# Recurrent stage: five high halves on GpSimd, the exponentials ahead of the roots, one gate block ahead of a gate chunk

## The chip, the cores and the metric

The kernel runs on one core of a Trainium2 chip. The metric is the device time in microseconds, the median of three runs: 1562.83 (1562.11 to 1563.29).

## The reference, cut to what matters

Two transformer-like blocks of depth 2 run over 256 tokens of width 1024. The change touches one stage, the gated linear recurrence of the first block, and the projection behind it:

```python
gate_br, rec = jnp.split(h @ w_in, 2, axis=-1)
gate_br = gelu(gate_br);  xc = causal_depthwise_conv(rec, conv_w, conv_b)
r = sigmoid(block_diag_linear(xc, w_r, b_r));  i = sigmoid(block_diag_linear(xc, w_i, b_i))
log_a = -8.0 * r * softplus(-lam);  a = exp(log_a)
mult = sqrt(-expm1(2.0 * log_a));  u = mult * (i * xc)
hs = linear_recurrence(a, u)            # h = a_t * h + u_t
return (hs * gate_br) @ w_out
```

Everything is in fp32.

## The kernel before, in words

**Weights.** All weights pass through one stream of 576 units of 128x1024 fp32. A unit is loaded (in pairs, from SP's queue) into the ring `raw` of 8 slots. A high half `w_hi` of it is made by ScalarE (`split_hi`, L480 to L492, a Copy with output rounded to the matmul's format), and VectorE makes the low half `w_lo = raw - w_hi` (`split_lo`, L1018 to L1025). A product of a 128x128 block with 256 tokens is three matmuls: hi by hi (L1822), hi by lo of the operand (L1828), lo by hi (L1829). A load into a slot waits for the low halves of the slot's last pair; `split_hi` waits for the load and for TensorE to be done with the unit that held the slot 8 units earlier (the semaphore `unit_used`).

**Order.** Each engine has its own order, written out by hand. `pump_to(c)` on ScalarE and on VectorE makes the halves of all units up to c that aren't made yet; the calls stand between the stage's own steps.

**The stage.** Units `gates`+0 to +11 are: eight chunks of the gate projection (`gate_chunk`, 8 products each, units +0, 1, 2, 4, 8, 9, 10, 11), two units with the blocks of w_r (+3, +6) and two with those of w_i (+5, +7). `r_block(n)` and `i_block(n)`, n = 0 to 3, are 4 products each. Behind them come the `wout` units +0 to +7, 8 products each. TensorE's order is: chunks 0, 1, 2, r_block 0, chunk 3, r 1, i 0, r 2, i 1, r 3, i 2, chunk 4, i 3, chunk 5, chunks 6 and 7 interleaved by output bank, wout 0 to 7. `r_block(n)` needs `xc_lo(n)` of VectorE (L1336), wout k needs `y_lo(k // 2)` (L1389).

**ScalarE** does for each quarter n of the features: the high half of the convolved input (`xc_hi`, L651), the tanh of the r gate and of the i gate (L659, L664), tanh and exp for the decay (`r_tanh`, `decay`, L671, L676), the root (`mult_root`, L680), the gelu (L684) and the high half of the result (`y_hi`, L688). Tanh and exp share a function table; the root and the gelu each load one of their own.

**VectorE** does the convolution (L1349, 6 instructions a quarter), `xc_lo`, the scaled gate input (`mixed_in`, L1357), `mult_square` (L1364, L1365), `read_gate` (L1370, which reads a bank of the gate projection from PSUM), `recur` (L1377 and two scans, L1379), `y_full` (L1384) and `y_lo` (L1389). `y_full(b)` needs `gelu(b)`; `gelu(b)` needs `read_gate(b)`; `recur(b)` needs `mult_root(b)`.

**GpSimd** only issues a few DMAs and makes one sum of squares, later on (L446, L448).

Of the kernel before, what the change touches and what calls it, by code (L numbers as in the profile page):

```python
# [38 lines left out]
UNIT = 1024  # L39
RING = 8  # L40
# [117 lines left out]
GATE_UNITS = [AT["gates"] + _n for _n in (0, 1, 2, 4, 8, 9, 10, 11)]  # L158
R_UNITS = [AT["gates"] + _n for _n in (3, 6)]
I_UNITS = [AT["gates"] + _n for _n in (5, 7)]  # L160
STEPS = {"ffn0": 0, "ffn1": FFS, "ffn2": 2 * FFS, "ffn3": 3 * FFS, "mlp0": 4 * FFS, "mlp1": 4 * FFS + MLS}


class Signals:


    def __init__(self, sem):
# [10 lines left out]
        self.out_done = sem("out_done")  # L178

        self.hi_ready = sem("hi_ready")  # L180
        self.lo_ready = sem("lo_ready")
        self.unit_used = sem("unit_used")

# [130 lines left out]
def build(nc, stream, x_in, ctx_in, small, consts, late, poolmat, tab, out):  # L314
    with ExitStack() as es:
# [118 lines left out]
        @block.gpsimd  # L434
        def _(pool):
            gp = nc.gpsimd

            def sum_squares(n):

                m = POOL_SUMS[NORMS[n]]  # L440
                for b in range(1, 4):
                    pool.wait_ge(S.sq_ready, 4 * n + b + 1)
                    if b > 1:
                        pool.wait_ge(S.pool_sum, 3 * m + b - 1)
                    a = buf[4][:, half(0)]
                    gp.tensor_tensor(a, a, buf[4][:, half(b)], ALU.add).then_inc(S.pool_sum, 1)  # L446
                pool.wait_ge(S.pool_sum, 3 * m + 3)
                gp.tensor_tensor(buf[4][:, 0:T], buf[4][:, 0:T], buf[4][:, T:2 * T], ALU.add).then_inc(S.ctx_ssq, 1)  # L448


            pool.wait_ge(S.hi_ready, 4)
            pool.dma_start(cst[:, CC["tri"]:], consts[:, CC["tri"]:]).then_inc(S.mixer_consts_in, 16)
            for n, name in enumerate(NORMS):
                if name == "ctx":

                    pool.wait_ge(S.acc_ready, 4 * ACC["wout"] + 4)
                    pool.dma_start(buf[3][:, :], ctx_in).then_inc(S.ctx_in, 16)
                if name == "woe":

                    pool.wait_ge(S.acc_ready, 4 * ACC["ffn3"] + 4)  # L460
                    pool.dma_start(buf5[:, 0:NLATE], late).then_inc(S.late_in, 16)

                    pool.dma_start(buf[2][:, 0:TABW], tab[0]).then_inc(tab_in[0], 16)
                    pool.wait_ge(S.mixed_lo, 4)
                    pool.dma_start(buf[4][:, 0:TABW], tab[1]).then_inc(tab_in[1], 16)
                if name == "pool":

                    pool.wait_ge(S.na_max, 16)
                    pool.dma_start(buf[2][:, :], poolmat[:, 0:8 * T]).then_inc(S.poolmat_in, 16)
                    pool.dma_start(buf[0][:, 1024:2048], poolmat[:, 8 * T:]).then_inc(S.poolsum_in, 16)  # L470
                if name in POOL_SUMS:
                    sum_squares(n)
# [3 lines left out]
        def _(act):  # L476
# [2 lines left out]

            def split_hi(c):  # L480

                if c in MOD_UNIT:
                    return
                slot = c % RING
                act.wait_ge(raw_landed[slot // 2], 16 * (c // RING + 1))
                before = [n for n in range(c - RING, -1, -RING) if n not in MOD_UNIT]
                if before:

                    act.wait_ge(S.unit_used, SPLIT[before[0]] + 1)
                u = slice(slot * UNIT, (slot + 1) * UNIT)  # L490
                sc.activation(w_hi[:, u], raw[:, u], ACT.Copy).then_inc(S.hi_ready, 1)  # L491

            def pump_to(last):
                while nxt[0] <= min(last, UNITS - 1):
                    split_hi(nxt[0])
                    nxt[0] += 1
# [164 lines left out]
            def i_gate(n):  # L661
                act.wait_ge(S.i_ready, n + 1)
                for k in (2 * n, 2 * n + 1):
                    sc.activation(ig[:, k, :], bank2(n)[:, k % 2, :], ACT.Tanh, bias=ty("bih", k), scale=0.5).then_inc(S.i_read, 1)  # L664

            def r_tanh(n):
                if n == 0:
                    act.wait_ge(S.ms_psum, NRM["ffn0"] + 1)
                act.wait_ge(S.r_read, 2 * n + 2)
                for k in (2 * n, 2 * n + 1):  # L670
                    sc.activation(tn[:, k, :], r[:, k, :], ACT.Tanh, bias=ty("sp4", k), scale=ty("sp4", k)).then_inc(S.lru_tanh, 1)  # L671

            def decay(n):
                act.wait_ge(S.lru_tanh, 2 * n + 2)
                for k in (2 * n, 2 * n + 1):
                    sc.activation(r[:, k, :], r[:, k, :], ACT.Exp, bias=ty("nsp4", k), scale=ty("nsp4", k)).then_inc(S.lru_decay, 1)  # L676
# [5 lines left out]
            def gelu(b):  # L682
                act.wait_ge(S.acc_read, 4 * RD["gate"] + b + 1)
                sc.activation(buf[1][:, half(b)], buf[1][:, half(b)], ACT.Gelu_apprx_tanh).then_inc(S.gelu_done, 1)  # L684

            def y_hi(b):
                act.wait_ge(S.lru_y, b + 1)
                sc.activation(u_hi[:, 2 * b:2 * b + 2, 0:T], ck(buf[1])[:, 2 * b:2 * b + 2, :], ACT.Copy)\  # L688
                  .then_inc(S.operand_hi, 2)
# [1 line left out]
            xc_hi(0)  # L691
            pump_to(AT["gates"] + 7)
            xc_hi(1)
            pump_to(AT["gates"] + 8)
            sc.preload_act_table_set("exp_and_others")
            r_gate(0)
            r_tanh(0)
            xc_hi(2)
            pump_to(AT["gates"] + 9)
            r_gate(1)  # L700
            decay(0)
            xc_hi(3)
            i_gate(0)
            r_gate(2)
            pump_to(AT["gates"] + 10)
            i_gate(1)
            r_gate(3)
            r_tanh(1)
            i_gate(2)
            decay(1)  # L710
            r_tanh(2)
            i_gate(3)
            pump_to(AT["gates"] + 11)
            decay(2)
            r_tanh(3)
            decay(3)
            sc.preload_act_table_set("sqrt_and_others")
            mult_root(0)
            mult_root(1)
            gelu(0)  # L720
            pump_to(AT["wout"])
            y_hi(0)
            gelu(1)
            pump_to(AT["wout"] + 1)
            mult_root(2)
            mult_root(3)
            pump_to(AT["wout"] + 2)
            y_hi(1)
            gelu(2)
            gelu(3)  # L730
            pump_to(AT["wout"] + 3)
            pump_to(AT["wout"] + 5)
            y_hi(2)
            pump_to(AT["wout"] + 6)
            y_hi(3)
            pump_to(AT["ffn1"] + AHEAD - 1)
            gain_operand("ffn2_0", "wout", early=AT["ffn1"] + 8)
# [269 lines left out]
        def _(dve):  # L1007
# [10 lines left out]
            def split_lo(c):  # L1018

                if c in MOD_UNIT:  # L1020
                    modulate(c, *MOD_UNIT[c])
                    return
                dve.wait_ge(S.hi_ready, SPLIT[c])
                u = slice((c % RING) * UNIT, (c % RING + 1) * UNIT)
                ve.tensor_tensor(w_lo[:, u], raw[:, u], w_hi[:, u].bitcast(F32), ALU.subtract).then_inc(S.lo_ready, 1)  # L1025

# [43 lines left out]
            def pump_to(last):  # L1070
                while nxt[0] <= min(last, UNITS - 1):
                    split_lo(nxt[0])
                    nxt[0] += 1
# [281 lines left out]
            def mixed_in(b):  # L1355
                dve.wait_ge(S.i_read, 2 * b + 2)
                ve.scalar_tensor_tensor(buf[3][:, half(b)], buf[3][:, half(b)], 1.0, buf[0][:, half(b)], ALU.add, ALU.mult)\  # L1357
                  .then_inc(S.mixed_in, 1)

            def mult_square(b):  # L1360

                dve.wait_ge(S.lru_decay, 2 * b + 2)
                dve.wait_ge(S.mixed_in, b + 1)
                link(ve.tensor_tensor(buf[0][:, half(b)], buf[2][:, half(b)], buf[2][:, half(b)], ALU.mult))  # L1364
                ve.scalar_tensor_tensor(buf[4][:, half(b)], buf[0][:, half(b)], 1.0, buf[4][:, half(b)],  # L1365
                                        ALU.add, ALU.mult).then_inc(S.lru_m2, 1)
# [29 lines left out]
            mult_square(1)  # L1396
            pump_to(AT["gates"] + 11)
            mixed_in(2)
            mixed_in(3)
            mult_square(2)  # L1400
            mult_square(3)
            read_gate(0)
            recur(0)
            read_gate(1)
            y_full(0)
            pump_to(AT["wout"])
            y_lo(0)
            pump_to(AT["wout"] + 1)
            recur(1)
            read_gate(2)  # L1410
            y_full(1)
            pump_to(AT["wout"] + 2)
            y_lo(1)
            read_gate(3)
            recur(2)
            pump_to(AT["wout"] + 3)
            y_full(2)
            recur(3)
            y_lo(2)
            pump_to(AT["wout"] + 5)  # L1420
            y_full(3)
            pump_to(AT["wout"] + 6)
            y_lo(3)
            pump_to(AT["ffn1"] + AHEAD - 1)
            update_and_operand("wout", "ffn1", "ffn2_0", 1.0)
# [357 lines left out]
        def _(pe):  # L1783
# [257 lines left out]
            i_block(1, 0)  # L2041
            r_block(3, 1)
            i_block(2, 1)
            gate_chunk(4, 0)
            i_block(3, 0)
            gate_chunk(5, 2)

            unit_ready(GATE_UNITS[7])
            for n in range(NC):
# [571 lines left out]
```

## Time and profile before

| | before |
|---|---|
| time, median of 3 runs | 1562.83 us |
| span of the profiled execution (first to last instruction) | 1560.5 us |
| TensorE busy | 1523.2 us (98%) |
| VectorE busy | 1164.3 us (75%) |
| ScalarE busy | 785.1 us (50%) |
| GpSimd busy | 9.6 us, 15 instructions |
| mean granted TensorE clock | 0.995 |

The profiled execution's own time isn't given apart from the runs; its span is 2.3 us below their median, which is the time around the first and the last instruction. Busy time of TensorE is modelled from pipelined matmuls, so what counts there is where it stood idle. The recurrent stage lies between about 232 and 299 us of the span.

### The profile page before, as it was taken

How to read it: one execution, taken by the hardware profiler on the slowest of the kernel's cores; microseconds unless marked ns; L12 is line 12 of the kernel's file. 1: busy time of each engine (PE TensorE's matmuls, PEld its weight loads, DVE VectorE, ACT ScalarE, POOL GpSimd, SP SyncE). 2: the span in 40 equal slices, each digit the busy share in tenths (PEclk: the TensorE clock that was granted, in tenths of full speed). 3: DMA queues.
4: the chain of work that ended last, by engine and by line, in shares of the span. 5: the costliest groups of instructions: out<-in, count | busy, mean ns of one | idle time of the engine just before them, and what ended most of it. 6: DMA issues, size and time to landing. Idle time of an engine off the chain costs nothing.

```text
span 1560.5 us, 28953 instructions
## 1 busy us (share of the span) xinstructions
PE 1523.2 (98%) x11842; PEld 1463.9 (94%) x11842; DVE 1164.3 (75%) x1675; ACT 785.1 (50%) x1127; POOL 9.6 (1%) x15
## 2 busy tenths in 40 slices
PE   7999999999999999999989999999999999899998
PEld 7999998999999899999769999987799999899998
DVE  7887788978877858787767877774768887686563
ACT  5444458643435633445765343454654544454542
POOL 0000000000000100000000000000000000000000
PEclk9999999999999999999999999999999999999999
DMA  7656652646664537666233666643345767336540
GB/s 286 230 225 261 228 221 91 243 154 249 226 253 187 226 114 284 250 236 249 81 135 109 263 250 248 247 161 135 102 149 219 268 265 274 136 126 226 189 163 28
DMA packets 43735, 311.57 MB, mean 200 GB/s; under 512 B 4848, under 2 KB 5104, under 8 KB 6512
## 3 DMA queue, kind: packets, MB, share of 16 engines
q1 hardware_dynamic: 42048, 303.33, 51.7%
q0 software_dynamic: 1008, 5.73, 1.0%
q8 instruction: 75, 1.23, 0.3%
q10 hardware_dynamic: 576, 1.05, 0.2%
q14 instruction: 28, 0.23, 0.0%
HBM read 309.05 MB, written 1.05 MB: 199 GB/s over the span
## 4 chain that ended last, share of the span: by engine, by line
PE 67%; DVE 10%; ACT 3%; issue 1%; DVEq 0%; ACTq 0%
PE psum L1822 18%; PE psum L1828 18%; PE psum L1829 18%; DVE w_lo L1025 5%; PE psum L2066 3%; PE psum L2072 3%; PE psum L2071 3%; DVE buf L1034 2%; ACT w_hi L491 2%; PE psum L1899 1%; DVE buf L1195 1%; PE psum L2385 1%; PE psum L2396 0%; PE psum L2315 0%; DVE buf L1198 0%
## 5 line engine op out<-in xcount | busy, mean ns | idle before, releaser
L1822 PE MATMUL psum<-u_hi,w_hi 128*128 128x256 f32 (+1 forms) x2288 | 658.1, 288 | 17.1 <-DVE u_lo L1117 9.6
L1025 DVE TENSOR_TENSOR w_lo<-raw,w_hi 128x1024 fp32r<-128x1024 f32 x480 | 564.5, 1223 | 115.6 <-ACT w_hi L491 115.4
L1828 PE MATMUL psum<-u_lo,w_hi 128*128 128x256 f32 (+1 forms) x2288 | 650.1, 284 | 0.0
L1829 PE MATMUL psum<-u_hi,w_lo 128*128 128x256 f32 (+1 forms) x2288 | 649.9, 284 | 0.0
L491 ACT ACTIVATE w_hi<-raw 128x1024 fp32r<-128x1024 f32 x480 | 477.3, 1046 | 71.0 <-PE psum L1822 59.0
L1822 PEld LDWEIGHTS psum<-u_hi,w_hi 128*128 128x128 f32 x2288 | 440.9, 193 | 21.5 <-DVE w_lo L1025 9.7
L1828 PEld LDWEIGHTS psum<-u_lo,w_hi 128*128 128x128 f32 x2288 | 441.0, 193 | 0.4
L1829 PEld LDWEIGHTS psum<-u_hi,w_lo 128*128 128x128 f32 x2288 | 440.8, 193 | 0.0
L1822 PE MATMUL psum<-hid_hi,w_hi 128*128 128x256 f32 x1220 | 346.2, 284 | 1.8 <-issue 1.2
L1828 PE MATMUL psum<-hid_lo,w_hi 128*128 128x256 f32 x1220 | 345.2, 283 | 0.0
L1829 PE MATMUL psum<-hid_hi,w_lo 128*128 128x256 f32 x1220 | 345.1, 283 | 0.0
L1822 PEld LDWEIGHTS psum<-hid_hi,w_hi 128*128 128x128 f32 x1220 | 234.2, 192 | 2.4 <-issue 1.4
L1828 PEld LDWEIGHTS psum<-hid_lo,w_hi 128*128 128x128 f32 x1220 | 234.2, 192 | 0.1
L1829 PEld LDWEIGHTS psum<-hid_hi,w_lo 128*128 128x128 f32 x1220 | 234.2, 192 | 0.0
L549 ACT ACTIVATE buf<-buf 128x256 f32<-128x256 f32 x88 | 36.8, 418 | 313.3 <-DVE buf L1195 313.3
L1034 DVE SCALAR_TENSOR_TENSOR buf<-raw,tiny,buf 128x512 f32<-128x512 f32 x196 | 143.4, 748 | 4.9
L596 ACT ACTIVATE buf<-buf,tiny 128x256 f32<-128x256 f32 x64 | 29.1, 501 | 110.2 <-DVE buf L1260 110.2
L1195 DVE TENSOR_TENSOR buf<-psum,rstd 128x512 f32<-128x512 f32 x88 | 60.4, 686 | 22.1 <-PE psum L1829 21.6
L2066 PE MATMUL psum<-w_hi,u_hi 128*128 128x512 f32 x176 | 71.9, 408 | 0.9 <-DVE x L1135 0.9
L1198 DVE TENSOR_TENSOR buf<-buf 128x256 f32<-128x256 f32 x88 | 37.4, 425 | 42.6 <-ACT buf L549 42.6
L1200 DVE TENSOR_TENSOR hid_lo<-buf,hid_hi 128x256 fp32r<-128x256 f32 x88 | 37.4, 425 | 42.6 <-ACT hid_hi L551 42.6
L2072 PE MATMUL psum<-w_hi,u_lo 128*128 128x512 f32 x176 | 68.9, 391 | 0.0
(261 smaller groups left out, 1048.5 us busy)
## 6 DMA issues: line engine op xcount, KB each, us to landing
raw<-stream SPq DMA_DIRECT2D x288, 1024.0 KB, 5.0
buf<-tab POOLq DMA_DIRECT2D x2, 768.0 KB, 5.3
x<-x_in SPq DMA_DIRECT2D x2, 512.0 KB, 6.8
buf<-ctx_in POOLq DMA_DIRECT2D x1, 1024.0 KB, 9.4
buf<-poolmat POOLq DMA_DIRECT2D x1, 1024.0 KB, 5.3
out<-x ACTq DMA_DIRECT2D x4, 256.0 KB, 2.5
cst<-consts POOLq DMA_DIRECT2D x1, 864.0 KB, 9.0
buf<-late POOLq DMA_DIRECT2D x1, 640.0 KB, 4.2
```

The lines of the kernel that those rows point to most:

```text
L491: sc.activation(w_hi[:, u], raw[:, u], ACT.Copy).then_inc(S.hi_ready, 1)
L1025: ve.tensor_tensor(w_lo[:, u], raw[:, u], w_hi[:, u].bitcast(F32), ALU.subtract).then_inc(S.lo_ready, 1)
L1034: return ve.scalar_tensor_tensor(acc, w, c, acc, ALU.mult, ALU.add)
L1195: ve.tensor_tensor(t2.rearrange("p (k t) -> p k t", k=2), bank2(UP_BANK[j]), over2(rstd[:, :]), ALU.mult).then_inc(S.up_scaled, 1)
L1198: ve.tensor_tensor(h32[:, 0:T], sil, t2[:, T:2 * T], ALU.mult).then_inc(S.hid_f32, 1)
L1200: ve.tensor_tensor(ff_lo[:, j % 4, :], h32[:, 0:T], ff_hif[:, j % 4, :], ALU.subtract)\
L1822: ins = te.matmul(dst, w_hi[:, w], hi, start=first, stop=False, skip_group_check=True)
L1828: te.matmul(dst, w_hi[:, w], lo, start=False, stop=False, skip_group_check=True)
L1829: return te.matmul(dst, w_lo[:, w], hi, start=False, stop=last, skip_group_check=True)
L2066: ins = te.matmul(dst, u_hi[:, k, t], w_hi[:, w], start=first, stop=False)
L2071: te.matmul(dst, u_hi[:, k, t], w_lo[:, w], start=False, stop=False)
L2072: return te.matmul(dst, u_lo[:, k, t], w_hi[:, w], start=False, stop=last)
```

## The change

GpSimd makes the high halves of the units gates+8 to +11 and wout+0, as fp32 copies with the same waits; VectorE waits for GpSimd's semaphore for these. ScalarE no longer makes them. On ScalarE the order is now: all tanh and exp steps, then the four roots, then the gelus. On VectorE some steps trade places to go with that. On TensorE `i_block(3)` comes ahead of chunk 4.

```diff
+POOL_HI = [AT["gates"] + _n for _n in (8, 9, 10, 11)] + [AT["wout"]]
@@ gpsimd
+            def split_hi(c):
+                slot = c % RING
+                pool.wait_ge(raw_landed[slot // 2], 16 * (c // RING + 1))
+                before = [n for n in range(c - RING, -1, -RING) if n not in MOD_UNIT]
+                pool.wait_ge(S.unit_used, SPLIT[before[0]] + 1)
+                u = slice(slot * UNIT, (slot + 1) * UNIT)
+                gp.tensor_copy(w_hi[:, u], raw[:, u]).then_inc(S.pool_hi, 1)
+                if name == "ffn0":
+                    for c in POOL_HI:
+                        split_hi(c)
@@ scalar
-            pump_to(AT["gates"] + 8)        # likewise +9, +10, +11 further down
             ...
             i_gate(0)
             r_gate(2)
+            r_tanh(1)
             i_gate(1)
             r_gate(3)
+            decay(1)
             i_gate(2)
             r_tanh(2)
+            decay(2)
             i_gate(3)
             r_tanh(3)
             decay(3)
             sc.preload_act_table_set("sqrt_and_others")
             mult_root(0)
             mult_root(1)
+            mult_root(2)
+            mult_root(3)
             gelu(0)
-            pump_to(AT["wout"])
             y_hi(0)
+            pump_to(AT["wout"] + 1)
             gelu(1)
-            pump_to(AT["wout"] + 1)
-            mult_root(2)
-            mult_root(3)
-            pump_to(AT["wout"] + 2)
             y_hi(1)
+            pump_to(AT["wout"] + 3)
             gelu(2)
             gelu(3)
             ...
@@ vector
-                dve.wait_ge(S.hi_ready, SPLIT[c])
+                if c in POOL_HI:
+                    dve.wait_ge(S.pool_hi, POOL_HI.index(c) + 1)
+                else:
+                    dve.wait_ge(S.hi_ready, ACT_HI[c])
             ...
             mixed_in(2)
+            mult_square(2)
             mixed_in(3)
-            mult_square(2)
+            pump_to(AT["wout"])
+            read_gate(0)
             mult_square(3)
-            read_gate(0)
             recur(0)
+            y_full(0)
             read_gate(1)
-            y_full(0)
-            pump_to(AT["wout"])
             y_lo(0)
+            recur(1)
             pump_to(AT["wout"] + 1)
-            recur(1)
+            y_full(1)
             ...
@@ tensor
             i_block(2, 1)
-            gate_chunk(4, 0)
             i_block(3, 0)
-            gate_chunk(5, 2)
+            gate_chunk(4, 1)
+            gate_chunk(5, 1)
```

## Rows read from the trace of the kernel before

**Rows 1.** The page: TensorE's totals, and the chain that ended last.
```profile
PE 1523.2 (98%) x11842; PEld 1463.9 (94%) x11842; DVE 1164.3 (75%) x1675; ACT 785.1 (50%) x1127; POOL 9.6 (1%) x15
PE psum L1822 18%; PE psum L1828 18%; PE psum L1829 18%; DVE w_lo L1025 5%; PE psum L2066 3%; PE psum L2072 3%; PE psum L2071 3%; DVE buf L1034 2%; ACT w_hi L491 2%; PE psum L1899 1%; DVE buf L1195 1%; PE psum L2385 1%; PE psum L2396 0%; PE psum L2315 0%; DVE buf L1198 0%
```

**Rows 2.** Waits, 250 to 262 us, then 262 to 300 us: total, times, longest.
```profile
DVE w_lo L1025 <- ACT w_hi L491: 3.8, 2, 2.4
...
PE psum L1822 <- DVE u_lo L1389: 3.5, 1, 3.5
DVE w_lo L1025 <- ACT w_hi L491: 0.5, 1, 0.5
```

**Rows 3.** Windows: length, busy us (xcount) of each engine, PEclk, DMA share, GB/s.
```profile
267.40:270.80 3.40, 0.00 (x0) 0.00 (x0) 3.31 (x5) 2.80 (x5) 0.00 (x0) 0.87 0.00 0
270.80:276.70 5.90, 5.86 (x27) 5.89 (x28) 5.40 (x7) 4.68 (x7) 0.00 (x0) 0.50 0.50 174
276.70:297.10 20.40, 19.79 (x165) 19.61 (x164) 20.21 (x25) 13.86 (x16) 0.00 (x0) 1.00 0.57 208
```

**Rows 4.** Timeline of TensorE's matmuls: start, us, engine, line; idle before in brackets.
```profile
260.83 0.28 PE L1829 MATMUL psum<-u_hi,w_lo 128*128 128x256 f32 x1
261.37 0.39 PE L1822 MATMUL psum<-u_hi,w_hi 128*128 128x256 f32 x1 [0.26 <-DVE w_lo L1025]
```

**Rows 5.** Timeline of VectorE in the stage.
```profile
241.46 0.68 DVE L1336 TENSOR_TENSOR u_lo<-buf,u_hi 128x512 fp32r<-128x512 f32 x1
242.07 2.45 DVE L1349 SCALAR_TENSOR_TENSOR buf<-buf,prm 128x256 f32<-128x256 f32 x6
244.44 1.21 DVE L1025 TENSOR_TENSOR w_lo<-raw,w_hi 128x1024 fp32r<-128x1024 f32 x1
245.92 0.69 DVE L1336 TENSOR_TENSOR u_lo<-buf,u_hi 128x512 fp32r<-128x512 f32 x1 [0.27 <-ACT u_hi L651]
...
250.04 0.69 DVE L1336 TENSOR_TENSOR u_lo<-buf,u_hi 128x512 fp32r<-128x512 f32 x1
...
254.03 0.69 DVE L1364 TENSOR_TENSOR buf<-buf 128x512 f32<-128x512 f32 x1
254.75 0.69 DVE L1365 SCALAR_TENSOR_TENSOR buf<-buf 128x512 f32<-128x512 f32 x1
...
265.09 0.68 DVE L1370 TENSOR_TENSOR buf<-psum,rstd 128x512 f32<-128x512 f32 x1
...
297.02 1.28 DVE L1135 SCALAR_TENSOR_TENSOR x<-psum,x 128x512 f32<-128x512 f32 x2
```

**Rows 6.** Timeline of ScalarE in the stage.
```profile
258.27 0.84 ACT L664 ACTIVATE buf<-psum,tiny 128x256 f32<-128x256 f32 x2 [1.09 <-PE psum L1829]
259.00 1.06 ACT L491 ACTIVATE w_hi<-raw 128x1024 fp32r<-128x1024 f32 x1
...
265.63 1.28 ACT L684 ACT_TABLE_LOAD   x1
266.93 0.63 ACT L684 ACTIVATE buf<-buf 128x512 f32<-128x512 f32 x1
```

**Rows 7.** Timeline of GpSimd, then of VectorE, around 540 us.
```profile
539.95 4.17 POOL L446 TENSOR_TENSOR buf<-buf 128x512 f32<-128x512 f32 x3 [241.59 <-ACT buf L509]
544.20 1.60 POOL L448 TENSOR_TENSOR buf<-buf 128x256 f32<-128x256 f32 x1
...
538.86 1.23 DVE L1025 TENSOR_TENSOR w_lo<-raw,w_hi 128x1024 fp32r<-128x1024 f32 x1 [0.81 <-ACT w_hi L491]
540.88 2.79 DVE L1470 TENSOR_SCALAR buf<-psum,tiny 128x512 f32<-128x512 f32 x4 [0.80 <-PE psum L2072]
543.59 3.30 DVE L1025 TENSOR_TENSOR w_lo<-raw,w_hi 128x1024 fp32r<-128x1024 f32 x2
```

**Rows 8.** Windows of a later stage, columns as in rows 3.
```profile
1195.00:1196.80 1.80, 0.03 (x2) 0.03 (x1) 1.72 (x7) 0.05 (x1) 0.00 (x0) 1.00 0.94 314
...
1198.30:1201.70 3.40, 3.40 (x18) 3.40 (x18) 2.45 (x4) 3.28 (x4) 0.00 (x0) 0.50 0.02 5
```

More of the change, by code:

```diff
@@ L160 @@
 I_UNITS = [AT["gates"] + _n for _n in (5, 7)]
+POOL_HI = [AT["gates"] + _n for _n in (8, 9, 10, 11)] + [AT["wout"]]
+ACT_HI = []
+for _c in range(UNITS):
+    ACT_HI.append((ACT_HI[-1] if ACT_HI else 0) + (_c not in MOD_UNIT and _c not in POOL_HI))
 STEPS = {"ffn0": 0, "ffn1": FFS, "ffn2": 2 * FFS, "ffn3": 3 * FFS, "mlp0": 4 * FFS, "mlp1": 4 * FFS + MLS}
@@ L180, in __init__ @@
         self.hi_ready = sem("hi_ready")
+        self.pool_hi = sem("pool_hi")
         self.lo_ready = sem("lo_ready")
@@ L480, in split_hi @@
             def split_hi(c):
-                if c in MOD_UNIT:
+                if c in MOD_UNIT or c in POOL_HI:
                     return
@@ L698, in _ @@
             xc_hi(2)
-            pump_to(AT["gates"] + 9)
             r_gate(1)
@@ L704, in _ @@
             r_gate(2)
-            pump_to(AT["gates"] + 10)
+            r_tanh(1)
             i_gate(1)
             r_gate(3)
-            r_tanh(1)
+            decay(1)
             i_gate(2)
-            decay(1)
             r_tanh(2)
+            decay(2)
             i_gate(3)
-            pump_to(AT["gates"] + 11)
-            decay(2)
             r_tanh(3)
@@ L719, in _ @@
             mult_root(1)
-            gelu(0)
-            pump_to(AT["wout"])
-            y_hi(0)
-            gelu(1)
-            pump_to(AT["wout"] + 1)
             mult_root(2)
             mult_root(3)
-            pump_to(AT["wout"] + 2)
+            gelu(0)
+            y_hi(0)
+            pump_to(AT["wout"] + 1)
+            gelu(1)
             y_hi(1)
+            pump_to(AT["wout"] + 3)
             gelu(2)
             gelu(3)
-            pump_to(AT["wout"] + 3)
+            pump_to(AT["wout"] + 4)
+            y_hi(2)
             pump_to(AT["wout"] + 5)
-            y_hi(2)
-            pump_to(AT["wout"] + 6)
             y_hi(3)
@@ L1398, in _ @@
             mixed_in(2)
+            mult_square(2)
             mixed_in(3)
-            mult_square(2)
+            pump_to(AT["wout"])
+            read_gate(0)
             mult_square(3)
-            read_gate(0)
             recur(0)
+            y_full(0)
             read_gate(1)
-            y_full(0)
-            pump_to(AT["wout"])
             y_lo(0)
+            recur(1)
             pump_to(AT["wout"] + 1)
-            recur(1)
+            y_full(1)
             read_gate(2)
-            y_full(1)
+            y_lo(1)
             pump_to(AT["wout"] + 2)
-            y_lo(1)
+            recur(2)
             read_gate(3)
-            recur(2)
             pump_to(AT["wout"] + 3)
@@ L1419, in _ @@
             y_lo(2)
+            pump_to(AT["wout"] + 4)
+            y_full(3)
             pump_to(AT["wout"] + 5)
-            y_full(3)
-            pump_to(AT["wout"] + 6)
             y_lo(3)
```

## The prediction, made before the changed kernel was timed

> **What bounds the kernel now.** I read the page first. TensorE is busy 98% of the span and the chain that ended last runs over its three matmul lines, with VectorE's low halves (L1025) next [rows 1]. So the whole is TensorE-bound, and the change can only move the places where TensorE stands still or where VectorE carries the chain. Then the waits and the windows of the stage. TensorE stands idle for 3.5 us ahead of the first wout product, for `y_lo(0)` [rows 2]. The granted clock is 1.0 before that, falls within this idle stretch to 0.50 (1.2 of 2.4 GHz) and stays there to 276.7 us [rows 3]: 27 matmuls in 5.9 us where full speed does 49. That looks like 3.5 + 2.6 us to be had. But from 276.7 to 297.1 us VectorE is busy for 20.21 of 20.40 us [rows 3], and what follows the stage, the update of x at 297.02, starts when VectorE gets to it. So from `read_gate(0)` at 265.09 to 297.02 VectorE, with 31.93 us of work, sets the end [rows 5]. The idle and slow stretches of TensorE lie beside it. In front of this VectorE waits 3.8 us for ScalarE's high halves [rows 2].
>
> **TensorE's schedule.** Matmuls start 0.12 us apart (165 in 19.79 us) [rows 3], so a chunk of 24 takes 2.88 us and a block of 12 takes 1.44. Counting back 240 matmuls from 260.95, the end of chunk 5 (its last matmul starts at 260.83) [rows 4], the gate projection starts at 232.15; chunk 1 at 235.0, chunk 2 at 237.9, r_block(0) at 240.8, r_block(1) at 245.1, i_block(0) at 246.55, r_block(2) at 248.0, r_block(3) at 250.9. The `xc_lo` that these need end at 242.15, 246.6 and 250.7 (start plus duration) [rows 5]: margins of 3.0, 1.4 and 0.2 us.
>
> **Exponentials first, input gate first.** ScalarE loses the five copies of 1.06 us [rows 6], all of which stood ahead of `y_hi(0)`; no step there is late any more. It gains two roots (0.62 us each) ahead of `gelu(0)`, and one pair of table loads of 1.28 us goes. `i_gate(3)`, which waited 1.09 us for TensorE [rows 6], gets its block 2.88 us earlier. None of this is on VectorE's path except through the waits. `mult_square(3)` now stands behind `read_gate(0)`, which waits for the first bank of chunks 6 and 7. With TensorE undisturbed that is 260.95 + 1.44 + 0.3 = 262.7: the 0.26 us wait for a low half at 261.37 [rows 4] goes, since VectorE has it by 258. Behind `read_gate(0)` VectorE's 31.93 us change thus: `mult_square(3)` comes in (0.72 from the start at 254.03 to that at 254.75, and 0.61, which is 0.69 less the overlap of 0.08 with the next: 1.33) [rows 5]; the low half of wout+0 goes ahead (-1.14); the wait of 0.5 for a high half [rows 2] goes. New waits come: `gelu(0)` now follows the fourth root. After `read_gate(0)` starts at t, VectorE's m2 is ready at t + 2.0; root 0.62, table load 1.28, gelu 0.63 [rows 6] make t + 4.55, while VectorE is done with `recur(0)` at t + 3.95: 0.6. Two `y_lo` wait 0.2 each for their high half, the low half of wout+2 0.35: together 1.3. Sum 31.93 + 1.33 - 1.14 - 0.5 + 1.3 = 32.9 us. Without any side effect the stage would end at 262.7 + 32.9 = 295.6 instead of 297.0: **-1.4 us**, far less than the waits that vanish.
>
> **The copies on GpSimd.** They start when their slots come free: +8 at 235.0, +9 at 237.9, +10 at 240.8, +11 and wout+0 at 246.55 (all data landed long before). For their own consumers, the low halves, that is early enough at any price up to 3 us. The question is what they do to VectorE. The trace has one such meeting. While GpSimd adds (544.20 to 545.80, and the tail of the sum before), two low halves take 3.30 us together instead of 2.35 (two of 1.23 that overlap by 0.1), and GpSimd's 256-column addition takes 1.60, more than its 512-column ones (4.17 for three, some 1.3 each with the waits between). Next to VectorE's L1470, which reads PSUM, those three ran undisturbed [rows 7]. So a GpSimd instruction that reads SBUF and a VectorE one with two SBUF inputs take turns: the second low half began at 545.13, was through 0.53 us late, and that is what the 512 reads of GpSimd need. The Trainium skill, "SBUF — State Buffer", section "Who interferes with whom", says it in these terms: the port pair that the two share is "an exclusive lock", and the later one "fully blocks". By that rule the trace agrees, with its 0.95 us lost.
>
> All of VectorE's work from 234 to 250.7 us, the convolution, the low halves and `xc_lo`, has two SBUF inputs, and VectorE is nearly full there. So each copy costs it the copy's reading time. Bounds from rows 7: 0.53 us (as the small addition), and 2.1 us (four times its elements). By reads it is 1024 against 512: **1.06 us**, which I take, as it is also about what a 512-column addition, with as many reads, takes as a whole. The Trainium skill ("GPSIMD Engine Reference", 4.1) calls a one-input operation roughly line-rate, which at the 1.2 GHz of its section 1 would be an estimate of 0.85 us and make the stage some 0.9 us shorter than with my value; no run here shows it yet.
>
> Three copies stand before `xc_lo(2)`: 246.6 - 0.3 (a wait for ScalarE that goes) + 3.2 = 249.5. That is past 246.55, so the other two get in front too: + 2.1 = 251.6. TensorE wanted it at 248.0: it stands still for 3.6 us in all at r_block(1) and (2). Behind it VectorE needs 2.40 + 1.13 + 0.61 = 4.15 us to `xc_lo(3)`, TensorE 2.88: 1.2 us more. r_block(3) starts at 255.8 instead of 250.9, a slip of 4.9. Nothing absorbs it: `read_gate(0)` waits for TensorE (262.7 + 4.9 = 267.6), and 267.6 + 32.9 = 300.5 against 297.0: **+3.5 us**. The idle stretch ahead of wout is still some 2.7 us (the chain from `read_gate(0)` to `y_lo(0)` takes 6.7 us, the rest of the chunks 4.0).
>
> **The clock.** Of idle stretches, the one of 3.5 us and one of 1.8 us were followed by 0.50, which lasted 5.9 busy us and 3.4 us [rows 3, 8]; a busy stretch of 3.4 us at it did 18 matmuls for 28, so 1.3 to 1.5 us lost. At r_block(2) there will be an idle stretch of over 3 us, where there was none. What is lost up to r_block(3) hides in its 1.2 us wait; what is lost later delays `read_gate(0)`. Bounds 0 and 3; I take 0.7.
>
> **Hidden or free.** The load of wout+4 and +5 waits for the low halves of gates+8 and +9: up to 5 us later, needed only after 275. GpSimd's queue behind the copies holds the ctx load, which waits for the end of wout anyway. The new wait of VectorE on GpSimd has the whole stage queued behind it, but is met 3 us ahead. The instruction on ScalarE that is displaced costs nothing there.
>
> **Sum.** -1.4 + 4.9 + 0.7 = +4.2 us on a span of 1560.5, that is 1564.7; the runs lie 2.3 us above the span, so 1567.0 (from the median, 1562.83 + 4.2).
>
> **Rivals.**
> (a) GpSimd's copy does not hold VectorE, as L1470 was not held, or VectorE's gaps take it up: then -1.4, 1561.4. Against it: L1470 has one SBUF input at most, the stage's work has two [rows 7].
> (b) Faster by more: VectorE gets back all its waits (3.8 + 0.5) and the clock is not lowered ahead of wout, so TensorE sets the end: -4.3, 1558.5. It decides from where VectorE has over 3 us of slack behind `read_gate(0)`; the windows show 0.2 [rows 3]. This is the case on the other side.
> (c) The copy is priced by elements, at 2.1 us. Then `xc_lo(0)` to `xc_lo(2)` are late, TensorE slips by 9 to 10 us: +8, 1571.
>
> **Chances.** Forecast mechanism, with a reading time of 0.7 to 1.6 us a copy: 0.62, its own range 1563.8 to 1569.5. (a) 0.22, (b) 0.09, (c) 0.07. A measurement of this kernel tells 0.2%, 3.1 us, from no change. Of the 0.62 some 0.15 falls below +3.1. So slower 0.47 + 0.07 = 0.54; within 0.15 + 0.22 = 0.37; faster 0.09. The range leaves out (b) and half of (c): 1560.9 to 1571.0.
>
> **What would show it.** Right: five GpSimd rows of 1.1 to 2 us between 235 and 252 us; convolution groups (L1349) of six that take 3.5 us instead of 2.45; idle of TensorE for `xc_lo` (L1336) of 4 to 5 us, and a low clock after it; `read_gate(0)` near 267.6 and the update of x near 301. Of the part without GpSimd: `i_gate(3)` without its wait, two table loads fewer, 0.6 us of VectorE's wait for the gelu, 2.7 us of idle ahead of wout. Wrong: L1349 groups still at 2.45 us beside GpSimd's rows (then rival a), or an x update that comes at 293 (rival b).

## The result: +1.4 us, where +4.2 was forecast

The changed kernel takes 1564.25 us (median of 15 runs, 1563.64 to 1567.63); the kernel before took 1562.89 us in the 15 runs beside it (1562.11 to 1563.79). The ratio is 1.0014 [1.0007, 1.0020]: 1.4 us slower by the medians, 2.2 us by the ratio. The interval lies above 1, so a small loss is likely, but both figures are less than the 0.2% (3.1 us) that the prediction took as the least difference that can be told. The profiled span grew from 1560.5 to 1561.9 us. Every run's time is 1.8 to 1.9 us above its span, not 2.3 as stands ahead of the prediction: the two profiled executions each took some 0.5 us less than the median of their kernel.

The page of the changed kernel: TensorE's totals and the chain hardly moved [rows 1]; GpSimd has its five new instructions (15 before, 20 now). Lines have shifted: low halves L1039 (were L1025), convolution L1363 (L1349), `xc_lo` L1350 (L1336), `read_gate` L1384 (L1370), the x update L1149 (L1135).
```profile
PE 1521.1 (97%) x11842; PEld 1461.5 (94%) x11842; DVE 1168.1 (75%) x1675; ACT 777.5 (50%) x1120; POOL 17.1 (1%) x20
PE psum L1836 18%; PE psum L1842 18%; PE psum L1843 18%; DVE w_lo L1039 5%; PE psum L2080 3%; PE psum L2086 3%; PE psum L2085 3%; DVE buf L1048 2%; ACT w_hi L508 2%; PE psum L1913 1%; DVE buf L1209 1%; PE psum L2399 1%; PE psum L2410 0%; PE psum L2329 0%; DVE buf L1212 0%
```
GpSimd's timeline in the stage (start, us, what, and in brackets the idle time before): the five copies.
```profile
235.69 1.03 POOL L463 CAST w_hi<-raw 128x1024 fp32r<-128x1024 f32 x1 [220.16 <-PE psum L1836]
238.55 1.53 POOL L463 CAST w_hi<-raw 128x1024 fp32r<-128x1024 f32 x1 [1.83 <-PE psum L1836]
241.43 1.04 POOL L463 CAST w_hi<-raw 128x1024 fp32r<-128x1024 f32 x1 [1.35 <-PE psum L1836]
247.19 3.89 POOL L463 CAST w_hi<-raw 128x1024 fp32r<-128x1024 f32 x2 [4.72 <-PE psum L1836]
```
VectorE's timeline, against [rows 5]. The convolution group that meets one copy, the first, takes 0.83 us more than the undisturbed 2.45; the group that meets the second and the third takes 1.60 more, the one that meets the fourth and the fifth 1.57 more. The two `xc_lo` (L1350) shown are the third and the last of four.
```profile
234.51 3.28 DVE L1363 SCALAR_TENSOR_TENSOR buf<-buf,prm 128x256 f32<-128x256 f32 x6
...
239.10 4.05 DVE L1363 SCALAR_TENSOR_TENSOR buf<-buf,prm 128x256 f32<-128x256 f32 x6
...
244.81 2.45 DVE L1363 SCALAR_TENSOR_TENSOR buf<-buf,prm 128x256 f32<-128x256 f32 x6
247.19 1.21 DVE L1039 TENSOR_TENSOR w_lo<-raw,w_hi 128x1024 fp32r<-128x1024 f32 x1
248.32 0.68 DVE L1350 TENSOR_TENSOR u_lo<-buf,u_hi 128x512 fp32r<-128x512 f32 x1
248.92 4.02 DVE L1363 SCALAR_TENSOR_TENSOR buf<-buf,prm 128x256 f32<-128x256 f32 x6
...
254.00 0.68 DVE L1350 TENSOR_TENSOR u_lo<-buf,u_hi 128x512 fp32r<-128x512 f32 x1
...
266.54 0.69 DVE L1384 TENSOR_TENSOR buf<-psum,rstd 128x512 f32<-128x512 f32 x1 [1.48 <-PE psum L1843]
...
271.27 0.69 DVE L1398 TENSOR_TENSOR buf<-buf 128x512 f32<-128x512 f32 x1 [0.80 <-ACT buf L701]
...
299.78 1.28 DVE L1149 SCALAR_TENSOR_TENSOR x<-psum,x 128x512 f32<-128x512 f32 x2
```
TensorE's timeline: r_block(2) and r_block(3) wait for `xc_lo`, and the first wout product stands behind 2.76 us of idle time instead of 3.5 [rows 2].
```profile
249.05 0.39 PE L1836 MATMUL psum<-u_hi,w_hi 128*128 128x256 f32 x1 [0.68 <-DVE u_lo L1350]
...
254.73 0.39 PE L1836 MATMUL psum<-u_hi,w_hi 128*128 128x256 f32 x1 [2.55 <-DVE u_lo L1350]
...
273.58 0.48 PE L1836 MATMUL psum<-u_hi,w_hi 128*128 128x256 f32 x1 [2.76 <-issue]
```
The windows of the changed kernel (columns as in rows 3). The first holds the waits ahead of r_block(2) and r_block(3) and the 4 us behind them: no low clock. The second is the first 2.7 us of the wout products, at the low clock. The other three answer to [rows 8]: the idle stretch of 1.8 us comes 2.8 us later here, and the stretch of 3.4 us behind it, which held 18 matmuls at 0.50 before, holds 31 at 1.00.
```profile
240.80:258.90 18.10, 14.87 (x122) 14.46 (x121) 17.86 (x28) 12.11 (x26) 4.93 (x3) 1.00 0.34 117
...
273.58:276.30 2.72, 2.72 (x13) 2.72 (x14) 2.65 (x4) 0.57 (x2) 0.00 (x0) 0.51 0.00 0
...
1197.80:1199.60 1.80, 0.05 (x1) 0.00 (x1) 1.75 (x7) 0.02 (x1) 0.00 (x0) 1.00 0.87 328
1199.60:1201.10 1.50, 1.50 (x13) 1.50 (x14) 0.58 (x1) 0.89 (x2) 0.00 (x0) 1.00 0.94 399
1201.10:1204.50 3.40, 3.40 (x31) 3.40 (x30) 2.45 (x4) 3.26 (x4) 0.00 (x0) 1.00 0.02 7
```

**Where the time went.** The profiles are best laid over each other by two marks on VectorE: the first row of the convolution's input (L1344, L1330 before) and the x update. The stage between them took 65.22 us before and 67.67 us now (**+2.45**). The rest, from the x update to the span's end, took 1263.48 us and now 1262.12 (**-1.36**), although nothing of it was changed; the low clock that is missing behind 1201 us is worth just this, as e7 shows below. With the start, 0.31 us later, that makes +1.4. The start means nothing by itself: over the 14 profiles the first mark lies between 231.34 (e8) and 232.69 us (e5), though no edit changes the work in front of it.

### The profile page after: what moved, and what is told of

The parts are those of the page before. It is cut to its first block, busy times and chain, and to the rows that moved or that the text cites. A ratio compares the mean times of both kernels' runs of the same rounds, so it can differ in the third digit from the quotient of the medians.

```text
span 1561.9 us, 28950 instructions
## 1 busy us (share of the span) xinstructions
PE 1521.1 (97%) x11842; PEld 1461.5 (94%) x11842; DVE 1168.1 (75%) x1675; ACT 777.5 (50%) x1120; POOL 17.1 (1%) x20
## 3 DMA queue, kind: packets, MB, share of 16 engines
q8 instruction: 75, 1.23, 0.3%
q10 hardware_dynamic: 576, 1.05, 0.2%
HBM read 309.05 MB, written 1.05 MB: 199 GB/s over the span
## 4 chain that ended last, share of the span: by engine, by line
PE 67%; DVE 10%; ACT 3%; issue 1%; DVEq 0%; ACTq 0%
PE psum L1836 18%; PE psum L1842 18%; PE psum L1843 18%; DVE w_lo L1039 5%; PE psum L2080 3%; PE psum L2086 3%; PE psum L2085 3%; DVE buf L1048 2%; ACT w_hi L508 2%; PE psum L1913 1%; DVE buf L1209 1%; PE psum L2399 1%; PE psum L2410 0%; PE psum L2329 0%; DVE buf L1212 0%
## 5 line engine op out<-in xcount | busy, mean ns | idle before, releaser
L1039 DVE TENSOR_TENSOR w_lo<-raw,w_hi 128x1024 fp32r<-128x1024 f32 x480 | 564.2, 1222 | 110.9 <-ACT w_hi L508 110.7
L508 ACT ACTIVATE w_hi<-raw 128x1024 fp32r<-128x1024 f32 x475 | 471.7, 1046 | 70.0 <-PE psum L1836 57.4
```

## The experiments

The stage and the rest, read off each profile by the same two marks, and the medians:
```
                     stage   to before   rest      median    ratio to before
before               65.22               1263.48   1562.89
changed              67.67    +2.45      1262.12   1564.25   1.0014 [1.0007, 1.0020]
e1_no_gpsimd         65.62    +0.40      1263.53   1563.28   1.0002 [0.9993, 1.0011]
e2_gpsimd_only       67.36    +2.14      1262.05   1563.64   1.0008 [0.9999, 1.0017]
e3_swap_only         64.01    -1.21      1261.98   1560.25   0.9985 [0.9976, 0.9994]
e4_fill              67.67    +2.45      1262.01   1564.49   1.0017 [1.0008, 1.0026]
e5_extra_copies      68.92    +3.70      1263.69   1566.84   1.0026 [1.0016, 1.0037]
e6_extra_memsets     65.23    +0.01      1263.64   1562.79   1.0002 [0.9993, 1.0011]
e7_before_fill_late  65.24    +0.02      1262.13   1561.29   0.9991 [0.9982, 1.0000]
e8_after_fill_late   69.15    +3.93      1262.01   1563.96   1.0009 [1.0000, 1.0019]
e9_swap_one_copy     62.75    -2.47      1262.20   1560.22   0.9982 [0.9973, 0.9991]
e10_two_copies       63.36    -1.86      1265.33   1559.12   0.9980 [0.9971, 0.9989]
e11_e9_fill_late     62.75    -2.47      1262.08   1558.73   0.9976 [0.9967, 0.9985]
e12_after_fill_r3    67.66    +2.44      1262.09   1564.43   1.0011 [1.0002, 1.0020]
```
Each median of an experiment is of 11 runs, of 8 for e5. The kernel before had 1562.78 us beside e1 to e4, 1562.38 beside e5 to e8 and 1562.71 beside e9 to e12; differences below are against these. Stage and rest come from one execution of each kernel, the profiled one.

**e1: the new orders without GpSimd.** The changed kernel, with the five copies back on ScalarE:
```diff
-POOL_HI = [gates+8, +9, +10, +11, wout]
+POOL_HI = []
             xc_hi(1)
+            pump_to(AT["gates"] + 8)        # likewise +9 behind xc_hi(2), +10 behind r_gate(2),
             ...                             # +11 behind i_gate(2), wout behind decay(3)
```


> The changed kernel with its new orders, but ScalarE makes the five high halves again (between its tanh and exp steps, the fifth ahead of the roots). Theory (GpSimd's copies hold VectorE): the convolution groups are back at 2.45 us, TensorE has no wait for xc_lo, read_gate(0) starts near 264 instead of 266.5, and the time falls by 2 to 2.5 us against the changed kernel, to about 0.2 us below the kernel before. Rival (the new orders cost the time): it stays at the changed kernel's time, 1.4 to 2.2 us above before. Second rival (the new orders are worth what ScalarE's freed time was meant to give): over 3 us below before.


The convolution groups were back at 2.45 and 2.46 us, TensorE had no wait for `xc_lo`, and the stage fell by 2.05 us against the changed kernel. But `read_gate(0)` came at 264.85 us, not near 264, since VectorE now waits 1.63 us for ScalarE's copy of wout+0; the x update came at 298.07, and the stage was 0.40 us longer than before. The time fell by 1.0 us, where 2 to 2.5 was expected, and is that of the kernel before. The new orders by themselves gain nothing once ScalarE has to make the copies.

**e2: GpSimd alone.** The kernel before, with the five copies on GpSimd and every order as it was:
```diff
+                if name == "ffn0":
+                    for c in POOL_HI:
+                        split_hi(c)         # GpSimd, as in the change
```


> The kernel before with one part alone: GpSimd makes the five high halves; all orders are the old ones. Theory: the convolution groups take 0.8 us more for each copy that falls into them, TensorE waits 3 to 4 us for xc_lo(2) and xc_lo(3), and the time is 2.0 to 2.7 us above before. Rival (VectorE's waits of 3.8 us for ScalarE's high halves, which go, take the loss up): the time is that of before, or up to 1 us below.


On VectorE's timeline the four groups take 3.28, 4.05, 2.45 and 4.02 us, to the digit those of the change:
```profile
234.28 3.28 DVE L1369 SCALAR_TENSOR_TENSOR buf<-buf,prm 128x256 f32<-128x256 f32 x6
...
238.88 4.05 DVE L1369 SCALAR_TENSOR_TENSOR buf<-buf,prm 128x256 f32<-128x256 f32 x6
...
244.58 2.45 DVE L1369 SCALAR_TENSOR_TENSOR buf<-buf,prm 128x256 f32<-128x256 f32 x6
...
248.70 4.02 DVE L1369 SCALAR_TENSOR_TENSOR buf<-buf,prm 128x256 f32<-128x256 f32 x6
```
r_block(3) waits the same 2.55 us. The loss of the stage (+2.14) is GpSimd's, and the expected 2.0 to 2.7 is met there; the time rose by only 0.9, since the low clock behind 1198 us was missing here too.

**e3: the swap alone.** The kernel before, with one edit in TensorE's order:
```diff
-            gate_chunk(4, 0)
             i_block(3, 0)
-            gate_chunk(5, 2)
+            gate_chunk(4, 1)
+            gate_chunk(5, 1)
```


> The kernel before with one part alone: i_block(3) ahead of chunk 4 on TensorE. Theory: ScalarE's wait of 1.1 us for that block goes, the high half of gates+11 behind it and with it VectorE's low half and all that follows come up to 1.3 us earlier, and as VectorE sets the stage's end, the time falls by 1.0 to 1.4 us. Rival (TensorE sets the end, the block's place is free): no change within 0.3 us.


Stage -1.21, as expected, and `read_gate(0)` comes at 263.89 instead of 265.09 us; the time fell by 2.5, more than the stage gives and more than the expected 1.0 to 1.4, again with the rest at 1262. VectorE still waits 1.23 us for ScalarE's copy of gates+11 in this version.

**e5 and e6: what of GpSimd's work holds VectorE.** The kernel before, with five GpSimd instructions that nobody needs at the places of the change's copies, in e5 copies between two idle buffers, in e6 memsets of one:
```diff
+                gp.tensor_copy(hid_lo_t, hid_hi_t)      # e5
+                gp.memset(hid_lo_t, 0.0)                # e6
```


> The kernel before; ScalarE still makes all high halves, and GpSimd in addition makes five copies of 128x1024 between two tiles that nobody reads at that time, with the waits of the changed kernel's copies. So only GpSimd's traffic is added. Theory (a GpSimd instruction that reads SBUF takes turns with VectorE's two-input ones): convolution groups 0.8 us longer per copy, TensorE waits 3.2 us in all for xc_lo, and the update of x starts about 3.7 us later than at 297.0, since no wait of VectorE for ScalarE is taken away. Rival (the loss comes from the semaphores or the waits for GpSimd, not from its traffic): no change.

> As the run with five extra copies, but GpSimd writes zeros of the same size instead, which reads nothing from SBUF. Theory (the reads collide): convolution groups stay at 2.45 us, no wait for xc_lo, the time of before within 0.5 us. Rival (any GpSimd access to SBUF holds VectorE): as with the copies, over 2 us later at the update of x.


GpSimd's first instruction, which is the only one beside its VectorE group, and that group, first in e5:
```profile
236.26 1.03 POOL L460 CAST hid_lo<-hid_hi 128x1024 fp32r<-128x1024 f32 x1 [220.79 <-PE psum L1837]
235.09 3.28 DVE L1364 SCALAR_TENSOR_TENSOR buf<-buf,prm 128x256 f32<-128x256 f32 x6
```
and in e6:
```profile
235.59 0.95 POOL L460 MEMSET hid_lo<- 128x1024 f32 x1 [220.17 <-PE psum L1837]
234.42 2.46 DVE L1364 SCALAR_TENSOR_TENSOR buf<-buf,prm 128x256 f32<-128x256 f32 x6
```
The memset, which writes the same tile and reads nothing, costs VectorE 0.01 us; the copy, which reads as well, 0.83. The x update comes at 301.61 us with the copies (stage +3.70) and 297.26 (+0.01) with the memsets. So it is neither GpSimd's waits nor its being busy with a write to SBUF. What the copy adds is the read; its rounded output format differs from the memset's too, and that was not tried apart. e5 costs more than the change, since ScalarE keeps its copies and nothing is gained in return.

**e4: the idle stretch ahead of wout.** The changed kernel, with 22 matmuls into a free bank where TensorE waits for `y_lo(0)`:
```diff
             pe.wait_ge(S.i_read, NC)
+            for n in range(22): te.matmul(psum[:, 0, 0:T], ...)
```


> The changed kernel with 22 extra matmuls of 256 columns (on data that is there, their result overwritten) in TensorE's idle stretch ahead of the first wout product, about 2.6 us. Theory (VectorE sets the end of the stage, the low clock there is hidden): the granted clock stays at 1.0 ahead of and in the wout products, the update of x starts where it did, near 299.8 us, and the median moves by less than 0.5 us. Rival (the low clock behind that idle stretch costs time): 1.3 us or more faster. If the runs of 1566 to 1567.6 among those of the changed kernel come from a low clock at this place, they vanish here; if they come from one at r_block(3), they stay.


The window behind the fill in the changed kernel, which held 13 matmuls at 0.51, holds 22 here at 1.00, and the x update comes at 299.99, stage +2.45 to a hundredth:
```profile
273.60:276.30 2.70, 2.62 (x22) 2.56 (x22) 2.63 (x5) 0.76 (x2) 0.00 (x0) 1.00 0.00 0
```
Neither the idle time nor the low clock behind it costs anything; VectorE carries that part. Three of 11 runs lay above 1565.8, as 5 of 15 of the changed kernel did: these do not come from here.

**e7 and e8: the low clock behind 1198 us.** The kernel before (e7) and the changed one (e8), with 14 matmuls in the wait of 1.8 us of [rows 8]:
```diff
+                        if j == 3:
+                            for n in range(14): te.matmul(psum[:, 4, 0:T], ...)
                         pe.wait_ge(S.up_scaled, h0 + j + 1)
```


> The kernel before with 14 extra matmuls, result overwritten, in an idle stretch of 1.8 us of TensorE at 1195 us, far behind the changed stage. In the kernel before, and in the run without GpSimd's copies, this stretch was followed by 3.4 us at half clock; in the changed kernel and three more, not. Theory (that low clock costs the kernel before 1.5 us, and the changed one is spared it by its place in time): this kernel has no low clock there and is 1.2 to 1.5 us faster than before. Rival: the same time within 0.3 us.

> The changed kernel with the same 14 extra matmuls at the same place. Theory: the changed kernel has no low clock there in most runs, so its median stays (within 0.4 us); against the kernel before with the same extra matmuls it is then slower by what the stage lost, 2.4 to 2.8 us, not by 1.4 to 2.2. Rival: it falls by as much as the kernel before does, and the difference stays near 1.4 to 2.2 us.


In e7, the stretch that held 18 matmuls at 0.50 holds 31 at 1.00, the rest falls to 1262.13 and the time by 1.1 (by the ratio 1.4):
```profile
1198.30:1201.70 3.40, 3.40 (x31) 3.40 (x30) 2.45 (x4) 3.26 (x4) 0.00 (x0) 1.00 0.04 12
```
In e8 the median falls by only 0.3. With the late stretch filled in both, the medians differ by 1563.96 - 1561.29 = 2.67 us, close to the stage's +2.45 and within the expected 2.4 to 2.8. This is no exact match: each of the two ratios is known to about 0.1% (1.5 us) either way. In e8's profile the low clock that I had predicted for r_block(3) is there, behind its wait, and the stage is 3.93 longer, 1.5 more than in the changed kernel:
```profile
252.00:254.50 2.50, 0.55 (x4) 0.55 (x5) 2.50 (x4) 2.30 (x6) 0.00 (x0) 1.00 0.20 23
255.20:258.60 3.40, 3.40 (x18) 3.40 (x18) 3.12 (x6) 2.66 (x8) 0.00 (x0) 0.50 0.65 272
```

**e12: the wait ahead of r_block(3) filled.** The changed kernel, with the wait `read("rec", n)` (VectorE has read a PSUM bank that the block will use) put ahead of that for `xc_lo`, and 16 matmuls into a free bank between them:
```diff
+                read("rec", n)
+                if n == 3:
+                    for m in range(16): te.matmul(psum[:, 3, 0:T], ...)
                 pe.wait_ge(S.xc_lo, n + 1)
-                read("rec", n)
```


> The changed kernel with 16 extra matmuls, result overwritten, in TensorE's wait of 2.6 us for xc_lo(3). Theory (in some runs the clock falls behind this wait and delays read_gate(0) by 1.4 us): the clock stays at 1.0 from 250 to 265 us, the median moves little (within 0.5 us) and fewer runs lie above 1565.8 than the 5 of 15 of the changed kernel. Rival (the high runs come from the later stretch at 1195 us alone): as many high runs as before.


The same two windows now:
```profile
252.00:254.50 2.50, 2.35 (x20) 2.15 (x18) 2.50 (x5) 1.30 (x4) 0.00 (x0) 1.00 0.00 0
255.20:258.60 3.40, 3.40 (x30) 3.40 (x30) 3.26 (x5) 3.40 (x10) 0.00 (x0) 1.00 0.86 308
```
Median and stage are the changed kernel's, but all 11 runs end by 1564.84. Of 15 runs of the changed kernel five lie above 1565.8, and four of the five show a mean granted clock of 0.993 or 0.996, where the ten others have 0.996 to 0.998. In some of its runs, then, a low clock probably strikes that its profiled run lacks. With either wait filled (e8, e12) no run of 11 lay that high, so which of the two it is in a given run, or whether it takes both, stays open: e8's profiled run has the low clock in the stage and still took only 1564.34 us. None of 11 against 5 of 15 is also thin evidence (were the fills without effect, a split as uneven as this would come about once in some twenty times).

**e9 and e11: one copy, put where it holds nobody.** e3, with GpSimd making gates+11 alone, and only behind `xc_lo(3)`; e11 has e7's fill as well:
```diff
+POOL_HI = [AT["gates"] + 11]
+                pool.wait_ge(S.xc_lo, 4)     # ahead of GpSimd's copy
```


> The kernel before with i_block(3) ahead of chunk 4, and one copy on GpSimd: the high half of gates+11, which there waits for xc_lo(3), so that it falls behind the convolution, into VectorE's wait of 1.2 us for just this half. Theory (a copy on GpSimd is worth its place only where VectorE has slack): no wait of TensorE for xc_lo, and the update of x starts 1.1 us before that of the run with the swap alone (295.8), near 294.7; time 1559.0 to 1559.6. Rival (GpSimd's copies are worth nothing wherever they stand): the time of the swap alone, 1560.25, or more.

> The kernel with the swap and one copy, with the 14 extra matmuls at 1195 us that keep the clock up there. Theory (that low clock is a matter of where in time the same idle stretch comes): the swapped kernel was spared it, so nothing more is won, within 0.4 us. Rival (it is there in most of its runs too): 0.8 to 1.5 us faster than without them.


GpSimd's copy and the x update in e9:
```profile
250.75 1.03 POOL L464 CAST w_hi<-raw 128x1024 fp32r<-128x1024 f32 x1 [235.29 <-DVE u_lo L1357]
...
294.50 1.28 DVE L1156 SCALAR_TENSOR_TENSOR x<-psum,x 128x512 f32<-128x512 f32 x2
```
The copy runs while VectorE waits for ScalarE's copy of gates+10 (1.4 us), so it costs nothing, and the 1.23 us wait of e3 is gone: stage -2.47, the x update at the expected place. The time was expected at 1559.0 to 1559.6; its median is 1560.22, the 1560.25 of e3, as the rival said. But it had two values: four runs at 1557.99 to 1558.46, with a mean clock of 0.999, and seven at 1560.04 to 1561.83, at 0.996 to 0.998. My expectation for e11, no more than 0.4 us, was wrong: with the late wait filled all 11 runs lie at 1558.02 to 1559.42, the median 1.5 us lower. So the one copy's gain of 1.26 us in the stage over e3 is shown in the profiles; in the time it was hidden by that low clock, and e3 with the late wait filled was not run. It is the best version here, 4.0 us below the kernel before by the medians and 5.5 below the changed one.

**e10: the change's orders with two late copies.** ScalarE makes gates+8 to +10, GpSimd gates+11 and wout+0 behind `xc_lo(3)`, and `mult_square(3)` is back ahead of `read_gate(0)`:
```diff
-POOL_HI = [gates+8, +9, +10, +11, wout]
+POOL_HI = [AT["gates"] + 11, AT["wout"]]
+                pool.wait_ge(S.xc_lo, 4)
-            read_gate(0)
             mult_square(3)
+            read_gate(0)
```


> The changed kernel's orders, with ScalarE making +8, +9 and +10 behind xc_hi(1) and xc_hi(2), GpSimd making gates+11 and wout+0 after xc_lo(3), and mult_square(3) ahead of read_gate(0) on VectorE. Theory: no wait for xc_lo; the gelu's table load no longer stands behind read_gate(0), so the idle ahead of wout falls to about 1.2 us and the clock stays at 1.0 there; update of x near 294.2, time 1558.8 to 1559.6. Rival (the new orders cost what they save): 1562 or more.


Stage -1.86 (1.0 less than expected), median 1559.12, within the expected range. The two copies did not find VectorE waiting: ScalarE's copy of gates+10 comes earlier in this order, so VectorE goes straight on behind `xc_lo(3)`, and its `mixed_in` (L1374) and `mult_square` (L1381) take 0.85 and 0.65 us more than their 0.68 and 0.69:
```profile
251.42 3.41 POOL L464 CAST w_hi<-raw 128x1024 fp32r<-128x1024 f32 x2 [236.09 <-DVE u_lo L1353]
...
252.40 1.53 DVE L1374 SCALAR_TENSOR_TENSOR buf<-buf 128x512 f32<-128x512 f32 x1
254.03 1.34 DVE L1381 TENSOR_TENSOR buf<-buf 128x512 f32<-128x512 f32 x1
```
From the first mark to `read_gate(0)` it takes 32.05 us, where e9 takes 30.80; the loss of 1.0 us against the expectation is in there. The wait ahead of wout was 1.80 us, not 1.2, and the clock behind it stayed at 1.00, as expected. Its profiled run was its longest, 1562.92, and holds two low stretches of at least 6.6 us. At the first the kernel before has 3.4 us [rows 8]; at the second, where TensorE has waited 3.4 us in both, the clock of the kernel before is 0.78 and 0.72 over two neighbouring windows of 3.4 us. Hence the rest of 1265.33:
```profile
1196.40:1203.00 6.60, 6.60 (x32) 6.60 (x33) 5.44 (x6) 4.59 (x6) 0.00 (x0) 0.50 0.20 60
1353.40:1360.00 6.60, 5.30 (x13) 4.26 (x14) 4.99 (x9) 3.76 (x5) 0.00 (x0) 0.50 0.08 12
```

## Why the prediction was right in its mechanism and too high in its size

- **The undisturbed chain was right.** `read_gate(0)` starts at 266.54; less the 0.31 of the later start and the 3.64 of slip (below) that is 262.59, against 262.7 in the sum. From there to the x update it took 33.24 us, against 32.9: the wait for the gelu was 0.80 instead of 0.6 and the rest is small. So this term is -1.2 instead of -1.4. It is GpSimd's relief of ScalarE that pays for it, since e1 shows +0.40 without. The listed signs of this part are in the trace: `i_gate(3)` has no wait, ScalarE has seven instructions fewer (1127 before, 1120 now: five copies and two table loads), and the idle time ahead of wout is 2.76 us.
- **The hold of VectorE was right, its size was not.** This is the mis-sized term. I scaled 0.53 us to 1.06 by the number of reads; the three windows that hold all five copies lose 0.83 + 1.60 + 1.57 = 4.0 us, **0.80 a copy**. The bounds of 0.53 and 2.1 held it. Undisturbed, a copy takes 1.03 us itself (e9), of which 0.80 to 0.83 are lost to VectorE. The estimate of 0.85 us from the Trainium skill ("GPSIMD Engine Reference", 4.1), which I had weighed and left aside, is closer to this loss than my 1.06; it would have shortened the slip by five times 0.21, about 1.05 us, not by the 0.9 that I wrote.
- **The slip follows.** The five copies cost 4.0 instead of 5.3, so `xc_lo(3)` came 1.4 us earlier than forecast and TensorE waited 0.68 + 2.55 = 3.2 instead of 4.8 us. In the kernel before, r_block(3) starts at 250.78 us, right at the end of `xc_lo(3)` (250.73), and not at 250.9: the margin of 0.2 us that I had counted was not there (the row of the kernel before stands below). So it slipped by 254.73 - 0.31 - 250.78 = 3.64 instead of 4.9. The split was off too. I had put the fourth and the fifth copy in front of `xc_lo(2)`; they started at 247.19, as soon as their slots were free, but VectorE's low half and `xc_lo(2)` went through at their usual 1.21 and 0.68 us, and the two copies were paid for in the group behind. So little of the wait stood at r_block(2), most at r_block(3).

```profile
250.78 0.39 PE L1822 MATMUL psum<-u_hi,w_hi 128*128 128x256 f32 x1
```

- **The clock in the stage** was predicted at 0.7, out of 0 to 3. In the profiled run it cost 0, in e8's 1.5. The low clock that I had listed as a sign was absent from the profiled run. Whether 0.7 is near the mean over all runs is not shown, since only profiled runs tell where the clock fell.
- **The stage** by these terms: -1.2 + 3.64 + 0 = +2.45, where the sum said +4.2. Rival (a), no hold, falls with e2 and e5; (c), 2.1 us a copy, with the same rows; (b) with e4, in which the idle stretch and the low clock ahead of wout vanish and nothing is gained.
- **What no step had:** the rest of the kernel, where -1.36 us came back. I had [rows 8] before me and used it as a price only, not as something that the change might move. e7 shows that this low clock is worth 1.1 to 1.4 us; with it filled away in both kernels (e7, e8) the medians are 2.7 us apart instead of 1.4.

In sum, 4.2 - 0.7 (clock) - 1.25 (slip) + 0.2 (chain) = +2.45 in the stage; -1.36 behind it and +0.31 before it give +1.4.

That the time fell into the range says little. The range of 1560.9 to 1571.0 would have held an unchanged time too, and I had given a clear slowdown 0.54 and a change too small to tell 0.37; the second came. What speaks for the mechanism is the rows: the longer groups, the waits for `xc_lo`, and e2, e5 and e6.

Not settled: why the same wait of 1.8 us is followed by the low clock in the profiles of before, e1, e5, e6 and e10, and not in those of the changed kernel, e2, e3, e4, e9 and e12. e9's two groups of runs say that it differs from run to run of one kernel.

## What to carry to other kernels

A copy on GpSimd is not free because GpSimd is idle: beside VectorE work with two SBUF inputs each 128x1024 copy took 0.8 us of VectorE, so it belongs where VectorE waits anyway (e9), and one has to look whether it still waits there once the order has changed (e10). Memsets of the same size cost it nothing here (e6). One operation moved past another on the engine that everyone waits for (e3) gained more than the whole rearrangement. When differences of 1 to 2 us count, measure the stage between two marks of the trace beside the total, for a low clock elsewhere can hide or feign as much, and filling the wait ahead of it (e7, e11) both removes it and shows it.

## What the runs showed of the hardware that was not expected

- Of GpSimd's two instructions of one size beside VectorE's two-input work, the memset (0.95 us) cost it 0.01 us and the copy (1.03 us undisturbed) 0.80 to 0.83: only the one that reads SBUF is felt, and for some four fifths of its time. That it is the reading one alone agrees with the Trainium skill ("SBUF — State Buffer", "Who interferes with whom"), by which such VectorE work contends with a GpSimd instruction that reads SBUF and not with one that only writes it. Both sides pay: the second copy took 1.53 us, the fourth and the fifth 3.89 together.
- The granted clock after the same wait of TensorE of 1.8 us, in the same code, was 0.50 for 3.4 us, 0.50 for at least 6.6 us (e10) or 1.00 throughout. Each stretch of 3.4 us cost 1.35 us (rest of e7) to 1.5 us (stage of e8) where TensorE set the end, and nothing where VectorE did (e4).
